# Low part of the queries stacked twice in the second pass of the stick-breaking scores

## The reference

```python
def stick_breaking_attention(q, k, v):
    """q, k, v: (B, H, S, dh). A[t,s] = beta_ts * prod_{s<j<t} (1 - beta_tj), s < t."""
    for i in range(seq // Q_BLOCK):
        ...
        z = jnp.einsum('bhqd,bhkd->bhqk', qb, kb).astype(jnp.float32) * scale
        strict = k_pos[None, :] < q_pos[:, None]
        log_beta = jax.nn.log_sigmoid(z)
        log_one_minus = jnp.where(strict, jax.nn.log_sigmoid(-z), 0.0)
        suffix = lax.cumsum(log_one_minus, axis=3, reverse=True) - log_one_minus
        weights = jnp.where(strict, jnp.exp(log_beta + suffix), 0.0)
        outs.append(jnp.einsum('bhqk,bhkd->bhqd', weights.astype(vb.dtype), vb))
```

## Time and profile before

| | us |
|---|---|
| median of three runs | 759.11 |
| profiled execution, device time | 759.82 |
| its span in the profile | 758.0 |
| TensorE matmul busy | 742.5 (98%) |
| VectorE busy | 358.1 (47%) |
| ScalarE busy | 318.5 (42%) |
| GpSimd busy | 337.1 (44%) |
| attention halves on TensorE | from 80.0 to about 299 |

### The profile page before, as it was taken

How to read it: one execution, slowest core, us unless ns; L and a number is a source line. 1 busy time by engine, 2 the same in 40 slices (tenths; PEclk the granted TensorE clock), 3 DMA queues, 4 the chain that set the end, 5 groups by cost and what they waited for, 6 DMA issues and landing times.

```text
span 758.0 us, 9588 instructions
## 1 busy us (share of the span) xinstructions
PE 742.5 (98%) x3520; PEld 621.6 (82%) x3520; DVE 358.1 (47%) x504; ACT 318.5 (42%) x430; POOL 337.1 (44%) x245
## 2 busy tenths in 40 slices
PE   7999999999999999999999999999999999999996
PEld 5888788888888888788899888888888888888884
DVE  3328669869868774355562112212221222221567
ACT  5223485674765765662123323332333243423410
POOL 6545154334434432794005444444444443654800
PEclk9999999999999999999999999999999999999999
DMA  8322412313314213762003232323232327332002
GB/s 294 108 88 101 122 56 80 117 56 116 106 56 118 78 57 111 278 225 80 1 1 112 83 111 83 111 83 111 83 111 83 110 83 271 118 103 91 29 29 83
DMA packets 24477, 78.33 MB, mean 103 GB/s; under 512 B 2944, under 2 KB 3328, under 8 KB 24448
## 3 DMA queue, kind: packets, MB, share of 16 engines
q1 hardware_dynamic: 24448, 77.94, 30.1%
HBM read 71.63 MB, written 2.10 MB: 97 GB/s over the span
## 4 chain that ended last, share of the span: by engine, by line
PE 95%; ACT 1%; DMA 1%; issue 1%; DVE 1%; POOL 0%; SPq 0%; DVEq 0%; POOLq 0%; ACTq 0%
PE ps L972 92%; PE ps L1066 2%; DMA sb_k<-qk_lo 1%; PE ps L1145 0%; DMA w_raw<-w_stream_in 0%; POOL w_lo L413 0%; ACT w_hi L473 0%; ACT fx_p L554 0%; DVE fx_nmax L786 0%; ACT L460 0%; ACT g_all L603 0%; SPq L340 0%; ACT wout_hi L606 0%; DVE x L907 0%; DVE bn_parts L879 0%
## 5 line engine op out<-in xcount | busy, mean ns | idle before, releaser
L413 POOL TENSOR_TENSOR w_lo<-w_raw,w_hi 128x512 fp32r<-128x512 f32 x220 | 294.4, 1361 | 370.7 <-ACT w_hi L473 365.0
L473 ACT ACTIVATE w_hi<-w_raw 128x1024 fp32r<-128x1024 f32 x109 | 115.5, 1060 | 225.8 <-DMA w_raw<-w_stream_in 225.8
L972 PE MATMUL ps<-x1T_hi,w_hi 128*128 128x512 f32 (+1 forms) x376 | 141.3, 376 | 0.0
L972 PE MATMUL ps<-x1T_lo,w_hi 128*128 128x512 f32 (+1 forms) x376 | 141.2, 375 | 0.0
L972 PE MATMUL ps<-x1T_hi,w_lo 128*128 128x512 f32 (+1 forms) x376 | 141.2, 375 | 0.0
L935 DVE SCALAR_TENSOR_TENSOR conv<-ps,col,conv 128x511 f32<-128x511 f32 (+1 forms) x44 | 33.0, 749 | 165.3 <-ACT conv L653 162.3
L972 PE MATMUL ps<-xT_hi,w_hi 128*128 128x512 f32 x264 | 105.9, 401 | 1.4 <-issue 1.0
L972 PE MATMUL ps<-xT_hi,w_lo 128*128 128x512 f32 x264 | 103.2, 391 | 0.0
L972 PE MATMUL ps<-xT_lo,w_hi 128*128 128x512 f32 x264 | 102.9, 390 | 0.0
L972 PEld LDWEIGHTS ps<-x1T_hi,w_hi 128*128 128x128 f32 x376 | 70.8, 188 | 12.9
L972 PEld LDWEIGHTS ps<-x1T_lo,w_hi 128*128 128x128 f32 x376 | 70.8, 188 | 12.7
(11 more groups left out here) (139 smaller groups left out, 1126.3 us busy)
## 6 DMA issues: line engine op xcount, KB each, us to landing
w_raw<-w_stream_in SPq DMA_DIRECT2D x109, 512.0 KB, 3.2
wout_raw<-w_out_in SPq DMA_DIRECT2D x8, 512.0 KB, 4.7
r_raw<-w_stream_in SPq DMA_DIRECT2D x5, 512.0 KB, 9.9
xT_raw<-xT_in SPq DMA_DIRECT2D x8, 256.0 KB, 6.5
x<-x_tok_in SPq DMA_DIRECT2D x4, 512.0 KB, 4.3
ln_rows<-rows_in SPq DMA_DIRECT2D x4, 512.0 KB, 5.5
out_dram<-x SPq DMA_DIRECT2D x8, 256.0 KB, 2.0
sb_q<-sb_q SPq DMA_DIRECT2D x8, 128.0 KB, 2.4
```

Of the source, the lines that this page charges most:

```text
L413: lo = nc.gpsimd.tensor_tensor(w_lo[:, slot, cs], w_raw[:, slot, cs], plain(w_hi[:, slot, cs]), ALU.subtract)
L473: nc.scalar.activation(w_hi[:, slot, :], w_raw[:, slot, :], ACT.Copy).then_inc(hi_ready, 1)
L972: return nc.tensor.matmul(out_, lhs, rhs, start=start, stop=stop, skip_group_check=True)
```

## The change

The low part of the queries gets two tiles of its own (`sb_ql[0]`, `sb_ql[1]`), one for each head of a pair, and SP copies each onto the other 64 partitions by one more DMA of 128 KB. The second pass of the scores then uses all 128 partitions: low part of the queries, twice, times high and low part of the keys, which adds the product low times low to the scores. TensorE waits for the two new DMAs by a semaphore of their own, `lo_stack_in`, between the two passes. VectorE writes the same instructions to other addresses. The numbers of matmuls and of their columns stay as they were.

```diff
-    qk_lo = at("qk_lo", [P, 2, SEQ], f32r, area_a + 22 * K)
+    sb_ql = [at("sb_ql0", [P, SEQ], f32r, area_a + 22 * K), at("sb_ql1", [P, SEQ], f32r, area_g + 24 * K)]
+    k_lo = at("k_lo", [P, SEQ], f32r, area_a + 24 * K)
...
+        lo_stack_in = sem("lo_stack_in")
...
-                    k_other = qk_lo[own, 1, :] if b == 0 else k_bias_rows[own, e, :]
+                    k_other = k_lo[own, :] if b == 0 else k_bias_rows[own, e, :]
                     sp.dma_start(plain(q[other, :]), plain(q[own, :])).then_inc(stack_in[b], 16)
                     sp.dma_start(plain(k[other, :]), plain(k_other)).then_inc(stack_in[b], 16)
+                if b == 0:
+                    for e in range(2):
+                        sp.dma_start(plain(sb_ql[e][other_rows(e), :]),
+                                     plain(sb_ql[e][rows_of(e), :])).then_inc(lo_stack_in, 16)
...
-                    lo = (qk_lo[r, j, :] if j < 2 else q_bias_rows[r, e, :] if j == 2 else fx_k[e][r, :])
+                    lo = (sb_ql[e][r, :], k_lo[r, :], q_bias_rows[r, e, :], fx_k[e][r, :])[j]
...
-                for q, k, first in ((sb_q[e][:], sb_k[e][:], True), (qk_lo[hd, 0, :], sb_k[e][hd, :], False)):
+                for q, k, first in ((sb_q[e][:], sb_k[e][:], True), (sb_ql[e][:], sb_k[e][:], False)):
+                    if not first:
+                        pe.wait_ge(lo_stack_in, (pair + 1) * 32)
                     for r in (3, 2, 1, 0):
                         o, width = SB_PS + QUERY_OFF[r], P * (r + 1)
                         product(ps[:, o:o + width], q[:, P * r:P * (r + 1)], k[:, 0:width], start=first and r > 0)
```

## The result

The changed kernel takes 763.3 us (median of six runs, 763.12 to 766.32) against 758.75 for the kernel before on the same chip: a ratio of 1.007, 95% interval [1.0054, 1.0086]. On a second chip it was 763.04 against 759.27, ratio 1.0048 [1.0032, 1.0065]. So it is slower, by 4.6 and 3.8 us. Forecast were 3.0 us, from 759.11 to 762.1: the direction was right and the rise was under-sized. Two executions in a slower state, one of the kernel before of 832 us and one of x_h0_as_changed of 1523 us, are in no ratio of this document.

A forecast was written before the change was run, and what follows sets the result against it. TensorE, holding 95% of the chain that ended last, was taken as the bound. Late loads +3.65, row savings -0.88 and half 0's wait +0.2 gave +3.0 us: 762.1 us from a median of 759.11, 8-in-10 range 759.4 to 763.8.

The forecast's parts named there:

- The rows, 0.22 us a half: TensorE's stick-breaking second pass: 128 rows instead of 64 save 0.22 us a half, bounds 0 and 0.27.
- Rival 3: Second pass on TensorE: the 64 rows don't cost the gaps, saving 0, total 763.2 us; chance 0.05.
- The late load and its chain, +3.65: SP's late weight load delays ScalarE, VectorE, then TensorE's fills: +1.29, +1.07, +1.29 us in halves 2, 4, 6.
- the 1.29: SP in halves 1, 3, 5: two added issues of 0.645 us each move the weight load by 1.29 us.
- Rival 1: SP's issues: the late load costs nothing, only the saving is left, 758.2 to 757.8 us; chance 0.13.
- Swallowed saving in halves 2, 4, 6; nothing caught up later: Fills of halves 2, 4, 6: the 0.22 us is lost in the wait, and engines late together recover nothing.
- The new wait in half 0, +0.2: TensorE's second pass in half 0 waits for the sixth stack DMA: +0.2 us, ends -0.22 and +0.4.
- The wait of 0.4 us at the second pass: Sign of a right forecast: TensorE waits some 0.4 us at half 0's second pass.
- the forecast 2.5: Sign of a right forecast: TensorE stands about 2.5 us before half 2's first fill.
- Rival 2: SP's long issue of 1.98 us in half 1 doesn't recur there; half 2 costs -0.1, total 760.7 us; chance 0.17.

The follow-up runs named there:

- x_h0_as_changed: Changed kernel with query copies issued before the load of weights in halves 1, 3 and 5, pair 0 stacked as in the changed kernel; ratio to kernel before 0.9978.
- x_rows128: Kernel before, second pass repeating the first on 128 rows with high queries, low-query product left out, no new DMA or wait; ratio 0.9978.
- the second profile of before: Kernel before run once more with no edit, for another profile; 758.49 us.
- the second profile of the changed kernel: Changed kernel run once more with no edit, for another profile; ratio to kernel before 1.0048.
- x_h0_long: Changed kernel, query copies before the weight load in halves 1, 3, 5; pair 0's six copies all behind its load, keys last; ratio to kernel before 0.9997.

## Why the prediction was wrong in size

Point by point, by its own steps:

- **The rows, 0.22 us a half.** Right: windows of 1.48 us, and x_rows128 gives 1.7 us by this alone. Rival 3 is out.
- **The late load and its chain, +3.65.** Right in mechanism and nearly in size. Against the second profile of before, the windows of halves 2, 4 and 6 rise by 1.27, 1.91 and 1.02, together 4.2; in the second profile of the changed kernel by 1.2, 1.8 and 1.2. Half 4 is the one that was more, by 0.8: ScalarE could take up its load 4.3 us after the issue, where it had been 3.4. I had said that a slower landing would add to the 1.29, and priced it at nothing. Why the load lands later in half 3 and not in 1 (3.7) stays open; the next load follows 0.9 us behind it in both. Half 6 was less, because the step read half 3's issues and took half 5 to be the same. In both profiles of before there is a gap inside half 5's stack, which is gone after the change, so this load moved by 1.05 and not 1.29:

```profile
238.27 0.59 SPq L341 DMA_DIRECT2D sb_k<-qk_lo  x1
239.28 0.46 SPq L340 DMA_DIRECT2D sb_q<-sb_q  x1
```

And half 2 nets less than its window shows (next point). From scores to scores the three halves take 0.76, 1.90 and 1.01 us longer than in the second profile of before, together 3.7. So the 3.65 came out, but in part by luck: 0.8 too little and 0.8 too much cancel. Rival 1 is out: the issues do hold SP.
- **Swallowed saving in halves 2, 4, 6; nothing caught up later.** Right in halves 4 and 6: from fill to next scores it takes 22.72 us before and after, where the clock is at 1.00. Not quite in half 2: a late fill there hides the wait for `fx_k` that the second profile of before has, so 0.5 us of the stand comes back (23.22 against 22.72).
- **The new wait in half 0, +0.2.** Right in size without the clock, but at another place: in the second profile the window is 1.68 against 1.73, and the stand before the first pass, which the step left as it was, is 1.22 against 0.97. x_h0_as_changed agrees with the size. The wait of 0.4 us at the second pass was 0.2 in the first profile's waits, and the second's show none.
- **What was not in the sum: the low clock.** This is the step that failed. The prediction took every matmul at the full clock, a term put at nothing, since the trace of before shows nothing else up to the last microseconds, also after a stand of 1.0 us. In each profile of the changed kernel one stand was followed by the low level: 1.4 us in half 0, with 0.2 more before the second pass, and 1.8 in half 4. Each cost 1.6 us (half 0: 1.03 up to the next scores and 0.6 in the window, beyond the rows and the wait). Twelve of the changed kernel's 14 executions have a mean clock that tells of a fall, so it is a regular term and no chance of two profiles. It is missing in a sum that lengthened three stands to 1.3 to 2.5 us. Between the second profiles, 5.0 us apart, the parts are 3.7 for the three late loads, 1.6 for the fall, 0.4 for the start and half 0, -0.9 for the rows, and 0.2 behind the halves: without the fall 3.4, near the forecast 3.0. In the medians the rise is 4.6 and 3.8, with some falls and long issues on the side of the kernel before as well.
- **The reference.** The sum was made against a profile with a chance stand of 1 us in half 2; the difference against it there was 0.1 and not 1.29, and the stand 1.3 us and not the forecast 2.5. The term of 1.29 can stand against the second profile, where the chain to half 2's fill has a slack of 0.1. Rival 2 came true in what it says of the trace: the long issue did not come again, and half 2 cost +0.1 against the first profile. But it took the long issue from the changed kernel and left it in the median of before, though nothing on record said that the executions behind that median had it; so its 760.7 was misread, and with it the range reached further down than up, where the miss lay.

The Trainium skill's page "TensorE: Matmul & The Clock Gate", section "HAM oscillation — how this bites in real kernels", says that waits between bursts of matmuls let TensorE's clock fall back and that the work after them starts slow. The runs here agree: in the profiles' halves, six falls, each after a stand of 1.4 to 2.5 us, and none after a stand of 1.3 us or less; six more stands of 1.4 to 2.2 us had none behind them. The waits of that section's example are longer, 3 to 5 us; here a fall stood behind one of 1.4. Had I weighed the rule against a forecast stand of 2.5 us, a low clock would have stood in the sum as a term with a chance.

## What to carry to other kernels

A DMA costs its issue time to whatever stands behind it on the issuing engine: look there for the load whose consumer has no slack, and put new copies where their source is ready first, not beside their relatives. When a forecast makes TensorE stand for 1.4 us or more, add the price of a low clock behind the stand, here 1.6 us, as a term with a chance; look at the mean clock of all executions, not of the profiled one alone. And take the reference of a sum from two profiles or more: each of the two here holds half a microsecond or more that the other hasn't got.

## What the runs showed of the hardware

A change from 128-row to 64-row matmuls and back costs 0.22 us: about 0.09 each way and 0.04 in the first matmul after it. Copies of 128 KB from SBUF to SBUF move at about 200 GB/s with the DMA engines nearly full (share 0.88), so six in a row hold them for some four microseconds: half 3 of the changed kernel, with DMA share and GB/s at the end of the row, and the load of weights that follows them:

```profile
187.00:188.00 1.00, 1.00 (x6) 0.84 (x5) 1.00 (x1) 0.00 (x0) 1.00 (x2) 1.00 0.88 207
191.00:192.00 1.00, 1.00 (x9) 0.91 (x8) 0.00 (x0) 0.00 (x0) 0.00 (x0) 1.00 1.02 410
```

An issue of a copy takes SP 0.60 us (0.47 for the first of a row) and now and then 1.3 to 2.0 for no reason that the profile shows (1.98, 1.32, 1.49 and 1.69 in halves 1 and 2 of four profiles). And whether the clock falls behind a stand of 1.4 to 2.2 us is not settled by the length of the stand: among the profiles stands of 1.43, 1.85, 2.13 and 2.19 us had a fall behind them, and 1.38, 1.41, 1.51, 1.60, 1.95 and 2.23 had not. Both stands of 2.5 had one. Of x_h0_long's eleven runs, with one stand of about 2.2 us, ten show the lower mean clock.
